# Sixteen attention units in retention's stage, GpSimd's first pages ahead of the last merges, semaphores cleared in runs

## The reference, cut to what matters

```python
def _retention(q, k, v, S0):                       # scan over chunks
    att = jnp.einsum('bihd,bjhd->bhij', qc, kc) * dm
    o = jnp.einsum('bhij,bjhe->bihe', att, vc) + jnp.einsum('bihd,bhde->bihe', qc, S) * q_dec
    S = S * s_dec + jnp.einsum('bjhd,bjhe->bhde', kc * k_dec, vc)
...
def _masked_softmax(s, mask):
    s = jnp.where(mask, s, -jnp.inf)
    m = jnp.max(s, axis=-1, keepdims=True)
    p = jnp.exp(s - m)
    return p / jnp.maximum(jnp.sum(p, axis=-1, keepdims=True), 1e-30)
...
# NSA on the prompt, for each head: softmax over compressed keys (o_cmp), over the
# selected keys (o_sel) and over the window (o_win); the three are summed with gates,
# and the sum is multiplied by the SiLU gate of the head group.
```

## Time and profile before

| | us |
|---|---|
| median of 3 runs | 2279.68 (2278.21 to 2285.9) |
| the profiled execution | 2280.29 |
| its span | 2278.7 |
| TensorE busy | 1985.9 (87%) |
| VectorE busy | 982.7 (43%) |
| ScalarE busy | 813.6 (36%) |
| GpSimd busy | 512.9 (23%) |
| retention, layer one, first to last instruction | 294.21 to 358.58 |
| delta attention, layer one | 359.75 to 641.98 |
| sample attention, layer one, from | 646.82 |

### The profile page before, as it was taken

How to read it: one execution, slowest core, us unless ns; L and a number is a source line. 1 busy time by engine, 2 the same in 40 slices (tenths; PEclk the granted TensorE clock), 3 DMA queues, 4 the chain that set the end, 5 groups by cost and what they waited for, 6 DMA issues and landing times. The chain is left out here.

```text
span 2278.7 us, 34709 instructions
## 1 busy us (share of the span) xinstructions
PE 1985.9 (87%) x11560; PEld 1354.8 (59%) x11560; DVE 982.7 (43%) x2408; ACT 813.6 (36%) x1894; POOL 512.9 (23%) x806
## 2 busy tenths in 40 slices
PE   6999957989968999996879999689898599999967
PEld 3644446778846676664336444567787467767633
DVE  2154355555533543443222542655654344444322
ACT  2211102334435655551222111033344366556502
POOL 0110011223243434420001100112232443444100
PEclk9999967999979999997989999689999799999979
DMA  5443111000068978853044520200000778888331
GB/s 190 157 162 118 37 41 25 1 11 1 5 162 185 211 169 205 197 131 125 0 161 149 198 80 28 51 16 1 11 1 21 182 185 181 198 208 197 92 125 42
DMA packets 173050, 242.55 MB, mean 106 GB/s; under 512 B 50714, under 2 KB 132282, under 8 KB 172192
## 3 DMA queue, kind: packets, MB, share of 16 engines
q1 hardware_dynamic: 143328, 146.81, 25.1%
q0 software_dynamic: 29536, 93.43, 15.6%
HBM read 223.23 MB, written 25.50 MB: 109 GB/s over the span
## 5 line engine op out<-in xcount | busy, mean ns | idle before, releaser
L611 PE MATMUL bank<-W,hT 128*128 128x512 f32 (+3 forms) x1152 | 444.4, 536 | 14.1 <-DMA W<-in_w_in 8.9
L611 PEld LDWEIGHTS bank<-W,hT 128*128 128x128 f32 x1152 | 213.9, 192 | 202.5 <-issue 173.3
L988 PE MATMUL bank<-XT,W 128*128 128x256 f32 (+1 forms) x768 | 246.9, 459 | 0.0
L1045 POOL DMA_DIRECT2D PS<-in_cache_nsa_kv x256 | 151.0, 590 | 270.4 <-issue 237.8
L1045 POOL DMA_DIRECT2D SHARED<-in_cache_nsa_kv x256 | 151.6, 592 | 184.5 <-DVE RP L958 103.3
L1273 ACT ACTIVATE Pr<-bank,mx 128x31 f32<-128x31 f32 (+4 forms) x192 | 85.7, 447 | 283.0 <-DVE mx L1461 282.8
L988 PEld LDWEIGHTS bank<-XT,W 128*128 128x128 f32 x768 | 136.0, 190 | 67.7 <-issue 50.4
L970 PE MATMUL bank<-CF,RP 128*128 128x128 f32 x1024 | 149.8, 295 | 24.2 <-DVE RP L958 24.0
L977 ACT ACTIVATE XT<-bank 128x512 f32<-128x512 f32 x256 | 141.1, 601 | 40.5 <-PE bank L970 40.4
L970 PEld LDWEIGHTS bank<-CF,RP 128*128 128x128 f32 x1024 | 126.6, 152 | 32.2 <-DVE RP L958 27.6
L1240 POOL TENSOR_TENSOR work<-UP,SHARED 128x512 f32<-128x512 f32 x56 | 72.9, 1307 | 249.0 <-DVE UP L1532 137.3
(11 more groups left out here) (426 smaller groups left out, 3470.8 us busy)
## 6 DMA issues: line engine op xcount, KB each, us to landing
SHARED<-in_cache_nsa_kv SPq DMA_DIRECT2D x256, 128.0 KB, 5.5
SHARED<-in_cache_nsa_kv POOLq DMA_DIRECT2D x256, 128.0 KB, 5.2
PS<-in_cache_nsa_kv SPq DMA_DIRECT2D x256, 128.0 KB, 5.5
PS<-in_cache_nsa_kv POOLq DMA_DIRECT2D x256, 128.0 KB, 5.0
W<-in_w_in SPq DMA_DIRECT2D x48, 512.0 KB, 3.7
XS<-scratch_conv_p POOLq DMA_DIRECT2D x24, 384.0 KB, 4.5
PW<-in_state_nsa_win SPq DMA_DIRECT2D x16, 512.0 KB, 3.8
Wo<-in_w_out SPq DMA_DIRECT2D x4, 2048.0 KB, 12.1
```

The lines of the kernel that those rows point to most:

```text
L611: return nc.tensor.matmul(bk((c * NTILE + t) % BANKS)[:, 0:b - a], hT[:, k, t * P:(t + 1) * P], W[:, k // 2, k % 2, 0:b - a], start=(k == ...
L988: mm = nc_(self.v).tensor.matmul(out, self.v['W1'][:, kv, s, :], seg[:, s], start=(s == 0), stop=(s == SEG // PAIRS - 1))
L1045: e.dma_start(where[side * HD:(side + 1) * HD, slot, :, :], A['cache_nsa_kv'][l, page].rearrange("(p r) a g d -> p r (a g d)", r=PAIRS)[:, ...
```

## The change

Three things are changed. (1) The 16 units of query tile 3 in branches 1 and 2 move from delta attention into retention. The unit code becomes a class, `Attend`, used by both stages, with the same three-slot delay; its groups there have two heads and two branches (4 units), and their merge writes `MIX`. The other 80 units stay in delta attention; the eight of tile 3 in branch 0 are merged four at a time and added to `MIX`. The tiles' order there is now 2, 0, 3, 1. Retention's steps are cut finer (`turn`, `att`, `back`, `norm`, `state`, `rows`, `halves`, `silu`, `second`: 29 steps) and the units are spread evenly among them, each engine in this one order. ScalarE now does exponentials in retention, ahead of its two SiLUs. (2) GpSimd asks for its first pages when the order comes to `("norm1", 3)`, ahead of the merges that stand behind it. (3) Semaphores with neighbouring numbers are cleared by one instruction.

```diff
+def clear(nc, sems):
+    numbers = sorted(s.num for s in sems)
+    first = numbers[0]
+    for a, b in zip(numbers, numbers[1:] + [None]):
+        if b != a + 1:
+            nc.gpsimd.sem_clear(range(first, a + 1))
+            first = b
...
-            for s in got:
-                nc.gpsimd.sem_clear(s)
+            clear(nc, got)
             nc.all_engine_barrier()
...
     TILES = (0, 1, 4, 2, 3)
-    ORDER = [("front", 0), ("front", 1)]
-    for i in range(NTILE):
-        ORDER += [("back", i)] + ([("front", i + 2)] if i + 2 < NTILE else []) + [("norm", i)]
+    STEPS = [("turn", 0), ("att", 0), ("turn", 1), ("att", 1), ("back", 0), ("turn", 2), ("att", 2), ("norm", 0), ("rows", 0), ("back", 1), ("turn", 3),
+             ("att", 3), ("norm", 1), ("back", 2), ("state", 0), ("state", 1), ("norm", 2), ("state", 2), ("state", 3), ("turn", 4), ("att", 4),
+             ("back", 3), ("norm", 3), ("halves", 0), ("halves", 1), ("back", 4), ("silu", 0), ("norm", 4), ("second", 0)]
+    heads = Attend.groups_of(EARLY_TILE, (1, 2), False)
+    NU = sum(len(g[1]) * len(g[2]) for g in heads)
+    ORDER, u = [("unit", 0), ("unit", 1)], 2
+    for j, step in enumerate(STEPS):
+        ORDER.append(step)
+        while u < NU and u < (NU + 1) * (j + 1) / len(STEPS) + 1:
+            ORDER.append(("unit", u))
+            u += 1
+    ORDER += [("unit", k) for k in range(u, NU + Attend.BACK)]
...
-    VM = sb(scope, "VM", [P, NB, 256])
+    VM = [U[2 + k][0:64, NQ:NQ + 512].rearrange("p (b c) -> p b c", b=2) for k in range(2)]
...
+                if what == "state":
+                    q, hp = divmod(i, 2)
+                    if i == 2:
+                        pe.wait(e, "sv1")
+                        values_by_row(1)
+                    pe.wait(e, f"sv{i}")
...
+class Attend:
+    DEEP, BACK = 2, 3
...
+    def pe_unit(self, e, u):
+        if u < self.NU:
+            self.scores(e, u)
+        if u >= self.BACK:
+            self.values(e, u - self.BACK)
+        if 1 <= u <= self.NU:
+            self.turn(e, u - 1)
+    def act_unit(self, e, u):
+        if u < self.NU:
...
+            nc.scalar.activation(self.Pr[:, u % self.DEEP, 0:n], self.bank(u)[:, 0:n], ACT.Exp, ...).then_inc(self.exped, 1)
+        if u - self.BACK in self.ends:
...
+            if k:
+                e.wait_ge(self.freed, k)
+            nc.scalar.activation(self.OB[:, 0:n], self.v['bk'](self.OUT)[:, 0:n], ACT.Copy).then_inc(self.merged, 1)
...
+    def pool_unit(self, e, u):
...
+        e.wait_ge(self.merged, k + 1)
+        e.wait_ge(self.scaled, k + 1)
+        link(nc.gpsimd.tensor_tensor(part, part, b_(self.fac[:, k % 2, 0:nh * nb], 2, [P, nh * nb, HD]), ALU.mult))
...
+EARLY_TILE = 3
+JOINT_TILES = (2, 0, 3, 1)
...
+    heads_of = sum([Attend.groups_of(EARLY_TILE, (0,), True) if qt == EARLY_TILE else Attend.groups_of(qt, (1, 2, 0), False) for qt in JOINT_TILES], [])
...
             for what, x in ORDER:
                 if (what, x) in mask_after:
                     mask(*mask_after[what, x])
-                if what == "unit" and x >= BACK and (x - BACK) % GROUP == GROUP - 1:
-                    merge((x - BACK) // GROUP)
-            dve.wait(e, "n33")
-            first_pages(e, A, l, v, 1)
+                if (what, x) == ("norm1", 3):
+                    dve.wait(e, "n33")
+                    first_pages(e, A, l, v, 1)
+                if what == "unit":
+                    attend.pool_unit(e, x)
...
-    for s in pc_rows[0] + pc_rows[1] + sel_rows[0] + sel_rows[1] + [win_rows]:
-        nc.gpsimd.sem_clear(s)
+    clear(nc, pc_rows[0] + pc_rows[1] + sel_rows[0] + sel_rows[1] + [win_rows])
```

More of the change, by code:

```diff
@@ L708, in retention @@
[L708 to L712, removed]
+    cps = []
+    for kv in range(2):
+        HT = sb(scope, "HTp", [HD, 64])
+        HS = sb(scope, "HSp", [HD, G, 32])
+        cps.append(Compress(v, 2, PG, RP, XT, HT, HS, KC, VC, ".p"))
+        cps[kv].HALVES, cps[kv].SECOND, cps[kv].TURNS, cps[kv].own = (0, 1), (0, 1), 0, True
@@ L724, in retention @@
+        if what == "halves":
+            pn += [f"H{i}.p"]
+            dn += [f"A{i}.p"]
+            an += [f"HT{i}.p"]
+        if what == "silu":
+            an += ["HS0.p", "HS1.p"]
+        if what == "second":
+            pn += ["C0.p", "C1.p"]
+            dn += ["C0.p", "C1.p"]
     dn += ["kc0", "kc1"]
     pn2 = [f"rg{t}" for t in TILES] + [f"{x}{t}" for t in TILES for x in ("gg", "vb")]
[L726 to L727 removed]
+    with stage(["dve_s", "act_s", "pe_s", "loaded", "gl", "rows", "small", "outs", "pool_s"] + Attend.SEMS) as \
+            (block, (dve_s, act_s, pe_s, loaded, gl, rows, small, outs, pool_s, *attend_sems)):
@@ L771, in _ @@
                 pool.done(e, f"vb{t}", nc.gpsimd.tensor_tensor(values, values, b_(u[:, GB:GB + H4], 2, [n, H4, HD]), ALU.mult))
+            for what, i in ORDER:
+                if what == "unit":
+                    attend.pool_unit(e, i)
         @block.scalar
         def _(e):
[L775 to L784, removed]
+            for what, i in ORDER:
+                if what == "unit":
+                    attend.act_unit(e, i)
+                if what == "rows":
+                    for k in range(2):
+                        cps[0].copy_out(e, act, pe, k)
+                if what == "halves":
+                    cps[i].half_copy(e, act, pe, dve, i)
+                if what == "silu":
+                    for kv in range(2):
+                        cps[kv].silu(e, act, dve, kv)
@@ L786, in _ @@
         @block.tensor
         def _(e):
[L788 to L800, removed]
@@ L802, in _ @@
-            for what, i, t in ORDER:
+            for what, i in ORDER:
+                if what == "unit":
+                    attend.pe_unit(e, i)
+                    continue
+                t = TILES[i]
                 u, n = U[t], ROWS[t]
                 QK, ATT, KDc = QK_[:, i % 2], ATT_[:, i % 2], KDc_[:, i % 2]
-                if what == "norm":
-                    beside(what, i)
-                if what == "front":
+                if what == "rows":
+                    dve.wait(e, f"att1{TILES[2]}")
+                    for k in range(2):
+                        cps[0].transposes(e, pe, act, dve, k)
+                if what == "halves":
+                    if i == 0:
+                        e.wait_ge(small, 13 * 16)
+                        dve.wait(e, f"att1{TILES[4]}")
+                    cps[i].halves(e, pe, act, i)
+                if what == "second":
+                    dve.wait(e, "A1.p")
+                    for kv in range(2):
+                        cps[kv].second(e, pe, act, dve, kv)
+                if what == "turn":
@@ L852, in _ @@
+                if what == "state":
+                    q, hp = divmod(i, 2)
+                    dve.wait(e, f"ss{i-1}m" if i else f"s1{TILES[1]}")
+                    if hp == 0:
+                        dve.wait(e, f"vm{q}")
+                    for k in range(2):
+                        mm = nc.tensor.matmul(bk(SU, 4)[:, 2 * k:2 * k + 2, :], KDc_[0:64, 0, hp * P:(hp + 1) * P], VM[k][:, :, hp * P:(hp + 1) * P],
                                               start=True, stop=True)
-                pe.done(e, f"su{t}", mm)
@@ L854, in _ @@
-                beside(what, i)
+                    pe.done(e, f"sv{i}", mm)
         @block.vector
@@ L994, in half_copy @@
         pe.wait(e, f"H{kv}{self.seq}")
-        if kv:
+        if kv and not self.own:
             dve.wait(e, f"A0{self.seq}")
```

464 lines of the change are left out of this document (251 added, 213 removed).

## The result

The changed kernel takes 2297.5 us (median of 14; 2283.43 to 2308.23) against 2282.37 for the kernel before (14 runs beside it): ratio 1.007, 95% interval 1.0054 to 1.0086. The forecast was 2238. The profiled execution took 2286.59 us, 6.3 more than that of the kernel before, so the trace shows 6.3 us of some 15; what is known of the rest stands under why the prediction was wrong.

A forecast was written before the change was run, and what follows sets the result against it. The kernel was taken as a sum of barrier-ended stages: retention a TensorE-VectorE chain, delta attention bounded by TensorE. +27 - 33 - 9.5 - 5.5 = -21 us a layer, -42 for two: 2238 us, range 2222 to 2255 (8 in 10: 2208 to 2270).

The forecast's parts named there:

- bounded by TensorE's work: Delta steps: TensorE is busy 234.6 of 261 us at clock 0.96, so removed work comes off almost whole.
- I add 5 us: Retention: allowance for the lower clock after two TensorE pauses of about 4 us, taking 87 to 92 us, +27.
- The walk: Retention: following VectorE's and TensorE's lists step by step at the clock's upper level gave 87 us.
- Rival (c): Retention: TensorE stays at the lower clock level, stage 126 us (+61), whole 2306 us; chance 0.09.
- -33: Delta attention: 16 units leaving save 36 us, smaller first units 1, less 4 allowed; net -33 us a layer.
- 4 us for thinner filling: Delta attention: 4 us allowed for steps following without a unit between, and for the smaller units.
- Rival (d): Delta attention: the chain of levels sets it, only half of 36 us comes off, whole 2268 us; chance 0.07.
- Pages: Behind `n33`: GpSimd's earlier issues gain 9.5 us a layer (8.4 to 11.4), depending on a possible extra 3 us hold.
- Semaphores: Stage boundaries: clearing in runs saves 5.5 us a layer; boundaries without transfers take 0.6 to 0.7 us.
- Rival (b): Stage boundaries: clearing a run costs as much as its members, -15 us a layer, whole 2250 us; chance 0.15.
- Rival (a): Retention: units fill the waits among finer steps, stage 79 us (+14), whole 2212 us; chance 0.17.
- Table loads: ScalarE in retention: loads for exponentials and SiLUs are hidden; a possible drain would add up to 2.8 us over both layers.

The follow-up runs named there:

- e4: The changed kernel with five useless products more at each of two places in retention where TensorE would wait; 2269.55 us, ratio 0.9951.
- e8: The changed kernel with two retention steps moved (rows, second split of the sample's values) and ScalarE's copy of outputs ahead of the exponential; 2255.29 us, ratio 0.9899.
- e1: The kernel before with only GpSimd's earlier page requests and semaphores cleared in runs, no units moved; 2251.42 us, ratio 0.988.

## Why the prediction was wrong

**What bounds the kernel** was read rightly, stage by stage. One word of it failed later: "bounded by TensorE's work" holds in part for the first 16 units (22.4 us came off for 30.3 of work), and not for the next 16 (none came off for 25.5).

**Retention, the step "I add 5 us".** This is the largest error. The walk at full level gave 87 us, and where the clock was up, it held: 88.7 us at a clock of 0.94 (e4, layer two, with ten products more), 86.0 at 0.90 with both mendings (e8). In part that is luck, as neither kernel has the order and the work that were walked through. But the lower level added 20.7 us, not 5. The walk had found both pauses of some 4 us and the earlier trace rows had shown what follows one; the price was set too low by 15.7, of which some 7 filled waits that the walk had counted as idle (17.8 idle, where the walk's 87 less 62 of work left 25), and TensorE's work was 3.5 larger (65.5 against 62). Together 12. Rival (c) had the mechanism, but with the whole stage at the lower level and +61 us; +39.6 lies between that and the forecast's +27.

**Delta attention, the term "-33".** Of the 37 us of work (36 and 1), 30.3 came off before `n33`: the tail behind `n33`, which other work covers, shrank as well (43 matmul instructions there instead of 64, the 44th of the row above being the sample stage's first, while the stretch ahead of it has 218 fewer). The "4 us for thinner filling" were 7.9: 5.2 more idle and 2.7 more at the lower level. Together that is 10.6 us short. Rival (d) came nearer in size (18 of the 36; 22.4 were measured), but the chain of levels would show as idle time alone. The runs show a second cause, that TensorE's clock gives back what its list loses: little in the changed kernel, some 22 us with 64 units or in the old order.

**Pages**: gain 10.1 against 9.5, by the mechanism as written; the possible hold of 3 us for GpSimd behind its issues did not come. **Semaphores**: the three boundaries gave 3.6 us, and pages and clears together 14.5 a layer (e1) against 15, so a run can't cost what its members do. The 5.5 counts the clears behind delta attention a second time, as the 12.6 us after `n33` already end in a short boundary; and "0.6 to 0.7 us" held for one of the boundaries only (0.68, 0.90, 1.73, and 1.6 behind the last merge). Rival (b) is out. Rival (a) is out: the finer steps left more waits, not fewer. **Table loads**: the trace has two more in each layer (at 386.67 and 400.64 in layer one), four in all, so the 2.8 us given for both layers would be 5.5; the sum without them stands, as the load at 386.67 begins 0.02 us behind the activation before it.

By the measured terms the sum is +3.5 a layer, +7 in all; the trace has +6.3. **What stays open**: the median lies 11 us above the profiled execution, and a second trace took 2288.7. The granted clock of the 14 runs goes from 0.922 down to 0.911 as the time rises from 2283 to 2308, and stages of one and the same code took 104.0 to 107.9 us (retention) and 239.4 to 248.2 us (delta attention up to `n33`; the 249.9 and 251.3 of an expectation are 246.8 and 248.2 by this count) in the traces above, mostly longer where the clock was lower. That fits the same cause; but the first `project`, which no run changed, ended between 289.9 and 297.9 us too, and no execution above 2289 us of this kernel was traced, so it is not shown. In delta attention of the changed kernel the lower level is in part carried over from retention; in layer one it falls at the same step with a wait of 1.80 us (470) and of 1.12 us (464, with the copy first). What brings it down at the other places was not found, and filling the stage's waits with nothing added was not tried.

The Trainium skill, TensorE: Matmul & The Clock Gate, section A second HAM failure mode: psum-queue depth-cycling, says that short pauses between groups of matmuls make TensorE go back and forth between its two levels and that throughput is lost by it. The prediction held that delta attention's rows disagree; with 80 and 64 units a larger share of the stage is at the lower level (mean clock 0.93 and 0.82, against 0.95 with 96), and there they agree. That short pauses are what does it there is not shown.

## What to carry to other kernels

Work taken from a TensorE that is 90% busy can come back as a lower clock: before counting a removed product at its full time, ask what else keeps TensorE busy at that place. In a stage that waits in turn on another engine, split its time into work at full level, what the lower level adds, and idle; if the second is large, filling the waits with products that nobody reads is a quicker gain (6 to 7 us of 64 here) than moving real work in. Put a step that another engine waits for ahead of a normalization that nobody waits for.

## What the runs showed of the hardware that was not expected

- Behind a pause of 4.67 us the level stayed at 0.50 for 19 us with TensorE busy in nearly all of them; with the pause filled it stayed at 1.00.
- 16 units less work on TensorE, some 25 us, left delta attention's length as it was (240.7 and 240.8, 242.4 and 238.6 us), and about as much work on useless products changed it by 3.8 on the mean (one execution of each).
- Clearing 17 semaphores in runs left a boundary of 0.68 us where single clears gave 1.75; GpSimd computes 0.01 us behind eight issues.
